# A recurrent tail walked by chunks, and attention's heads, softmax and value products placed inside the loop over cache pages

## The chip, the cores and the metric

The kernel runs on one core of one Trainium2 chip. The metric is the device time of one execution in microseconds (us); the median of several runs is compared. The engines are TensorE (PE; its weight loads are shown as PEld), VectorE (DVE), ScalarE (ACT), GpSimd (POOL) and SyncE (SP, which here only issues transfers). Each engine takes its instructions in a fixed order and waits on semaphores.

## What is computed

One inference step of a two-layer decoder for 256 prompt tokens and 8 sample tokens (T = 264 columns), model width 1024, all in float32. Layer 0 mixes by RWKV-7, layer 1 by latent attention, and after each a PEER expert mixer follows. Cut to what matters here:

```python
# layer 0, per head of 64, token by token (the kernel does it in 4 chunks of 64 tokens)
s = s*w_t - (s @ kk_t) * (kk_t*a_t) + v_t * k_t ;  y_t = s @ r_t
y = head_group_norm(y, ln_w, ln_b) + bonus ;  out = (y * g) @ w_out
# layer 1, prompt: 16 heads, two blocks of 128 queries, causal
o = softmax(scale*(q_nope k_nope^T + q_pe k_pe^T)) @ v
# layer 1, samples: 8 requests, each with 16 pages of 128 cached latents (256 wide) and keys (32 wide)
k_nope = rms_norm(ckv @ w_uk) * gain
s = scale*(q_nope . k_nope + q_pe . k_pe);  acc = softmax(s) @ ckv    # softmax over all pages and the new token
o = (acc/l) @ w_uv ;  out = o @ w_out
```

## The kernel before

Activations lie transposed, channels on partitions and the 264 tokens as columns, in 8 chunks of 128 channels. The weights stream through a ring of five tiles of 128x1024 (`ring`, 512 KB each), which SP loads in the order of use; an engine tells that a tile is free by `tile_used`. PSUM has eight banks of 128x512; TensorE's function `take(b)` waits until the last reader of bank b has raised `bank_free[b]`. `for_dve` and `for_act` tell a reader that a product is ready. `own` makes an engine wait for its own last instruction before it goes on, `tell` raises semaphores. `mm` (L714) and `turn` (a transpose, L773) issue TensorE's instructions; a float32 `mm` is two matmul instructions in the trace.

**Recurrent tail.** After the chunk products, `Pst` (the state of all 16 heads, 128x512) starts as chunk 0's. For each of chunks 1 to 3 TensorE makes 32 products of 64x64: for each half of the partitions what the old state adds to y, and then for each half the new state. The eight chunks c are walked inside one half. DVE adds the two y halves, then the two state halves, multiplies by the decay `lam`, and only then does the next chunk begin. Then come the group norm: head sums by a block matrix (8 products), centring on DVE, one square of all 128x2112 on DVE, head sums with 16 columns of weights (8 products), reciprocal and root, spreading back (8 products), gain, bias and gate on DVE over all chunks, and then the output product `rw_out` tile by tile with the sums of the next norm in it (`project_and_norm`).

**Prompt attention.** A loop of 17 turns over 16 heads: TensorE scores (4 products), DVE scale, mask and maximum, ACT two Exp, TensorE three `turn`s, ACT a copy, TensorE three value products, DVE the division. DVE prepares the masked query of the next head (`masked_query`). `o_row` is then turned back (16 `turn`s). After that TensorE makes the samples' query products (`qp`: 16 products with 16 columns, then 32 with 8), and only then may POOL load pages.

**Page loop.** 128 pages, 16 per request, four `cpT` buffers of the transposed page (192 KB, from `cache_t`), loaded by POOL when `page_used` tells that the page four earlier was scored. ACT rounds the page to its upper half (`page_upper`, two pages ahead), DVE makes the lower half (`page_lower`), TensorE makes the keys by 12 products of 512 columns into two banks, ACT squares both banks (`squares`), DVE sums the squares by head (`page_sums`) and copies the scores, which TensorE makes with the page as weights and 16 columns (3 products).

**Softmax and values.** After the last page: one root over all `SS` (128x2048), scores scaled, maxima over partitions (by a `turn` and a spread through a ones matrix), Exp, sums. Then 128 value products of 32 columns of weights by 256 columns, each with a natural page (`cpN`, 16 slots, 128 KB, from `cache_n`, issued in part by POOL and in part by ACT), copies of the rows on DVE, and 16 products that fold the rows back. Then `w_uv`, the output product `mla_out`, and layer 1's PEER.

Of the kernel before, what the change touches and what calls it, by code (L numbers as in the profile page):

```python
# [28 lines left out]
P = 128  # L29
# [3 lines left out]
NS = 8  # L33
# [136 lines left out]
def build(nc, x_t, shift_t, vecs, consts, wmasks, rope, wstream, sub_keys, mla_w, page_table, cache_t, cache_n,  # L170
          state, y_out, ckv_out, kpe_out, wkv_p_out, shift_out, wkv_s_out):
    ctx = ExitStack()
    with ctx:
# [103 lines left out]
        Pst = mis[:, 256:256 + 512].rearrange("p (c v) -> p c v", c=DC)  # L277
# [29 lines left out]
        def halves(name, cols, at):  # L307
# [70 lines left out]
        w_uv = A(2 * D, 2, D)  # L378
        w_ukT = A(DC * KVL, DC, KVL)
# [4 lines left out]
        qn_at = top[0]  # L384
        qn = A(N3, DC, T)
        kn_at = top[0]
        kn = A(N3, DC, T)
        qr = A(4 * T, 4, T)
        sqb = A(N3, DC, T)
        rs8 = A(N3, DC, T)  # L390
        vr_at = top[0]
        vr = A(2 * D, 2, D)
        o_t = A(N3, DC, T)
        qm = [A(512, 2, 256) for _ in range(2)]
        Sm = [A(384) for _ in range(2)]
        PTs = [A(384) for _ in range(2)]
        mxl = [A(8) for _ in range(2)]
        o_row = A(2 * D, 2, D)
# [10 lines left out]
        sqp = [o_row[:, j, :] for j in range(2)]  # L409
        small = A(10 * P, 10, P)  # L410
        cpT = [x.rearrange("p (a b) -> p a b", a=3) for x in Sm + PTs]
# [3 lines left out]
        acc_row = SS.rearrange("p g h -> p (g h)").rearrange("p (r n) -> p r n", r=NS)  # L415
        fold = small[:, 7, 0:HEADS]
        PR = rs8.rearrange("p c t -> p (c t)")[:, 0:NPG].rearrange("p (g h) -> p g h", h=HEADS)
        cpN = [a[:, i * KVL:(i + 1) * KVL] for a in (sqb.rearrange("p c t -> p (c t)"),
                                                     w_ukT.rearrange("p c n -> p (c n)")) for i in range(8)]

        uk_hi, uk_lo = halves("uk_hi", 2 * D, vr_at), halves("uk_lo", 2 * D, kn_at)
        pg_hi, pg_lo = halves("pg_hi", 4 * KVL, qn_at), halves("pg_lo", 4 * KVL, qn_at + 4 * KVL)
# [54 lines left out]
        yg_ready = sem("yg_ready")  # L477
        x_added = sem("x_added")
# [53 lines left out]
        rows_ready = sem("rows_ready")  # L532
        oall_ready = sem("oall_ready")

# [62 lines left out]
        def _(pool):  # L597
# [62 lines left out]
            pool.dma_start(wkv_p_out, Pst).then_inc(wkv_sent, 16)  # L660
# [13 lines left out]
            for n in range(4):  # L674
                page(pool, cache_t, n, cpT[n].rearrange("p a b -> p (a b)"), page_in[n])
            with pool.Fori(1, PAGES // 4) as it:
                for n in range(4):
                    pool.wait_ge(page_used, it * 4 + (n - 3))
                    page(pool, cache_t, it * 4 + n, cpT[n].rearrange("p a b -> p (a b)"), page_in[n])

            for n in POOL_SLOTS:
                page(pool, cache_n, n, cpN[n], natp_in[n])
            with pool.Fori(1, PAGES // NSLOT) as it:
                for n in POOL_SLOTS:
                    pool.wait_ge(natp_used, it * NSLOT + (n + 1 - NSLOT))
                    page(pool, cache_n, it * NSLOT + n, cpN[n], natp_in[n])
# [11 lines left out]
        def _(pe):  # L698
# [372 lines left out]
            for cc in range(1, NCH):  # L1071
                w.next(state_ready)
                cols = slice(cc * 64, cc * 64 + 64)
                for kind in range(2):
                    for h in range(2):
                        b = 2 * kind + h
                        take(b)
                        pr = slice(64 * h, 64 * h + 64)
                        for c in range(DC):
                            if kind == 0:  # L1080
                                last = mm(ps[pr, b, c * 64:(c + 1) * 64], Pst[pr, c, :], Rb[pr, c, cols])
                            else:
                                last = mm(ps[pr, b, c * 64:(c + 1) * 64], ETi[pr, c, cc, :], Pst[pr, c, :])
                        last.then_inc(for_dve, 1)

            w.next(ysm_back, 16)
# [6 lines left out]
            w.next(stat_ready)  # L1093
            head_roots(tmp_t, rs_rw)
            w.next(yg_ready)
            project_and_norm(TILES["rw_out"], y_t)
# [51 lines left out]
            for i in range(HEADS + 1):  # L1148
                if i < HEADS:
                    s, c = i % 2, i // 2  # L1150
                    w.next(qm_ready)
                    take(s)
                    for j in range(2):
                        o = ps[:, s, j * P:j * P + (j + 1) * P]
                        mm(o, qm[s][:, 0, j * P:(j + 1) * P], kn[:, c, 0:(j + 1) * P], True, False)
                        last = mm(o, qm[s][:, 1, j * P:(j + 1) * P], kp[:, 0:(j + 1) * P], False, True)
                    last.then_inc(for_dve, 1)
                if i >= 1:
                    h = i - 1
                    s = h % 2  # L1160
                    w.next(p_ready)
                    take(2 + s)
                    for k in range(3):
                        last = turn(ps[:, 2 + s, k * P:(k + 1) * P], Sm[s][:, k * P:(k + 1) * P])
                    last.then_inc(for_act, 1)
                    w.next(pt_ready)
# [71 lines left out]
            for n in range(PAGES):  # L1238
                req, p = n // NPAGE, n % NPAGE
                r = req % 2  # L1240
                if p == 0:
                    take(r)
# [1126 lines left out]
```

## Time and profile before

| | |
|---|---|
| runs | 3033.13, 3048.67, 3045.79 us; median 3045.79 |
| profiled execution | 3036.44 us, of which the profile's span is 3034.8 us |
| PE busy | 2768.0 us, 91% of the span |
| DVE busy | 1833.6 us, 60% |
| ACT busy | 1261.5 us, 42% |
| chain that ended last | PE 87%, DVE 6%, issue 2%, ACT 2%, DMA 1% |

The durations in the text are of the profiled execution. Granted clock means the share of full speed that TensorE was given: 1.00 is 2.4 GHz and 0.50 is 1.2 GHz; a value between is a mean over a stretch with both.

### The profile page before, as it was taken

The page shows a single profiled execution, that of the slowest core. Times are in us where ns is not written, and L with a number is a line of the kernel's source. Part 1 is how long each engine was busy: PE and PEld are TensorE (multiplying, and loading weights), DVE is VectorE, ACT ScalarE, POOL GpSimd, SP SyncE. Part 2 cuts the span into 40 slices and gives each one's busy share as a digit, 9 for nine tenths or more (in the row PEclk, how much of TensorE's full clock was granted, in tenths as well). Part 3 has the DMA queues.
Part 4 walks back from the last instruction along what each step waited for, and adds up shares of the span by engine and source line. Part 5 has one row for each costly group of instructions (what it writes and reads, how often), then busy time and mean ns, then how long its engine had stood idle before and what let it go on. Part 6 is the DMA issues. An engine that isn't in the chain of part 4 may idle for free.

```text
span 3034.8 us, 60374 instructions
## 1 busy us (share of the span) xinstructions
PE 2768.0 (91%) x22131; PEld 2522.1 (83%) x22131; DVE 1833.6 (60%) x3435; ACT 1261.5 (42%) x2565; POOL 181.6 (6%) x248
## 2 busy tenths in 40 slices
PE   8988699999999999975699999947999999999998
PEld 5777589999999999953488888822899999999998
DVE  5566457989985555525334444450579899855554
ACT  2333014467764444411233434410134677644443
POOL 0054000000000000000011111112000000000000
PEclk9999599999999999996689999975999999999999
DMA  4310034444445555530011122134345444455554
GB/s 163 120 43 27 15 119 152 162 163 157 160 148 181 182 182 180 205 144 0 1 42 57 57 58 58 57 89 135 121 150 167 160 154 160 148 182 182 181 180 139
DMA packets 112530, 378.00 MB, mean 125 GB/s; under 512 B 14617, under 2 KB 24090, under 8 KB 111842
## 3 DMA queue, kind: packets, MB, share of 16 engines
q1 hardware_dynamic: 88562, 322.17, 31.9%
q0 software_dynamic: 13424, 43.98, 4.9%
q10 hardware_dynamic: 10368, 9.44, 1.0%
q8 instruction: 119, 1.95, 0.3%
q14 instruction: 57, 0.47, 0.1%
HBM read 371.52 MB, written 4.01 MB: 124 GB/s over the span
## 4 chain that ended last, share of the span: by engine, by line
PE 87%; DVE 6%; issue 2%; ACT 2%; ACTq 1%; DMA 1%; DVEq 0%; POOLq 0%; POOL 0%; SPq 0%
PE ps L714 85%; DVE arena L1285 2%; ACT arena L1935 1%; DVE arena L1289 1%; ACTq L541 1%; DMA arena<-in_cache_n 1%; PE ps L1013 1%; PE ps L1008 1%; ACTq L542 0%; DVE ring_lo L1285 0%; PE ps L773 0%; DVE arena L1799 0%; ACT w_hi L1935 0%; DMA ring<-in_wstream 0%; DVE arena L1802 0%
## 5 line engine op out<-in xcount | busy, mean ns | idle before, releaser
L1285 DVE TENSOR_TENSOR ring_lo<-ring,w_hi 128x1024 fp32r<-128x1024 f32 x512 | 625.5, 1224 | 416.7 <-ACT w_hi L1935 413.3
L1935 ACT ACTIVATE arena<-ps 128x256 f32<-128x256 f32 (+19 forms) x981 | 397.5, 425 | 904.2 <-PE ps L714 823.5
L1935 ACT ACTIVATE w_hi<-ring 128x1024 fp32r<-128x1024 f32 x512 | 541.8, 1059 | 389.0 <-PE ps L714 388.6
L714 PE MATMUL ps<-arena 64*64 64x64 f32 (+11 forms) x5228 | 500.1, 275 | 143.4 <-DVEq L1282 54.6
L714 PE MATMUL ps<-x_hi,w_hi 128*128 128x264 f32 x2048 | 596.7, 291 | 15.5 <-DVE ring_lo L1285 15.5
L714 PEld LDWEIGHTS ps<-arena 64*64 64x64 f32 (+6 forms) x5228 | 391.5, 159 | 254.0 <-DMA arena<-in_cache_n 57.2
L714 PE MATMUL ps<-h_hi,w_hi 128*128 128x264 f32 x2048 | 580.1, 283 | 6.8 <-DVE ring_lo L1285 6.8
L714 PE MATMUL ps<-x_hi,ring_lo 128*128 128x264 f32 x2048 | 586.3, 286 | 0.0
L714 PE MATMUL ps<-x_lo,w_hi 128*128 128x264 f32 x2048 | 586.0, 286 | 0.0
L714 PE MATMUL ps<-h_lo,w_hi 128*128 128x264 f32 x2048 | 582.3, 284 | 0.0
L714 PE MATMUL ps<-h_hi,ring_lo 128*128 128x264 f32 x2048 | 581.9, 284 | 0.0
L1285 DVE TENSOR_TENSOR arena<-arena 128x512 f16<-128x512 f16 (+19 forms) x711 | 405.8, 590 | 46.8 <-ACTq L1940 31.3
L714 PEld LDWEIGHTS ps<-x_hi,w_hi 128*128 128x128 f32 x2048 | 390.7, 191 | 16.4 <-issue 16.3
L714 PEld LDWEIGHTS ps<-h_hi,w_hi 128*128 128x128 f32 x2048 | 385.7, 188 | 7.2 <-DVE ring_lo L1285 7.2
L714 PEld LDWEIGHTS ps<-x_lo,w_hi 128*128 128x128 f32 x2048 | 390.6, 191 | 0.0
L714 PEld LDWEIGHTS ps<-x_hi,ring_lo 128*128 128x128 f32 x2048 | 388.6, 190 | 0.0
L714 PEld LDWEIGHTS ps<-h_hi,ring_lo 128*128 128x128 f32 x2048 | 385.7, 188 | 0.0
L714 PEld LDWEIGHTS ps<-h_lo,w_hi 128*128 128x128 f32 x2048 | 385.7, 188 | 0.0
L714 PE MATMUL ps<-arena,ring 128*128 128x264 f32 (+2 forms) x1416 | 347.7, 404 | 25.3 <-DVE arena L1300 10.6
L714 PEld LDWEIGHTS ps<-arena,ring 128*128 128x128 f32 (+2 forms) x1416 | 275.4, 198 | 87.2 <-issue 20.1
L1935 ACT ACTIVATE arena<-arena 128x128 f16<-128x128 f16 (+5 forms) x586 | 200.2, 413 | 227.7 <-DVE arena L1289 121.2
L1849 DVE TENSOR_REDUCE arena<-arena 128x1024 f32 (+1 forms) x128 | 156.1, 1220 | 227.8 <-ACT arena L1935 227.8
(158 smaller groups left out, 2296.4 us busy)
## 6 DMA issues: line engine op xcount, KB each, us to landing
ring<-in_wstream SPq DMA_DIRECT2D x608, 512.0 KB, 3.3
arena<-in_cache_t POOLq DMA_DIRECT2D x128, 192.0 KB, 2.6
arena<-in_cache_n ACTq DMA_DIRECT2D x72, 128.0 KB, 2.4
arena<-in_cache_n POOLq DMA_DIRECT2D x56, 128.0 KB, 2.7
arena<-in_mla_w POOLq DMA_DIRECT2D x1, 3072.0 KB, 10.3
arena<-in_state POOLq DMA_DIRECT2D x4, 512.0 KB, 4.8
out_wkv_s<-arena POOLq DMA_DIRECT2D x4, 512.0 KB, 5.2
arena<-in_consts SPq DMA_DIRECT2D x1, 1408.0 KB
```

The source lines that it names most:

```text
L541: phys = eng.value_load(ptab[0:1, bass.ds(at, 1)], min_val=0, max_val=POOL - 1)
L714: return nc.tensor.matmul(out, lhsT, rhs, start=start, stop=stop, **kw)
L1008: last = nc.tensor.matmul(ps[par[f], 6 + x, q * CH:(q + 1) * CH], q4(XTs[x])[par[f], q, :], q4(Zs[x])[par[f], q, :], **acc)
L1013: last = nc.tensor.matmul(ps[par[f], 2 + x, q * CH:(q + 1) * CH], q4(Zs[x])[par[f], q, :], q4(XTs[x])[par[f], q, :], **acc)
L1285: return v.tensor_tensor(out, a, b, op)
L1289: v.reciprocal(x, x).then_inc(rsq_in, 1)
L1849: v.tensor_reduce(SS[:, bass.ds(at, 1), :].rearrange("p o h -> p (o h)"), sqp[n % 2].rearrange("p (h d) -> p h d", h=HEADS), AX.X, ALU.add ...
L1935: return nc.scalar.activation(out, in_, func, **kw)
```

## The change

Nothing of what is computed changes; order and placement do.

- The tail keeps a `Pst` for each chunk. Product by product it alternates between the two partition halves, puts both halves into one bank, and makes the new state first; reads of older states are placed behind it. DVE takes both halves in one operation. The norm goes chunk by chunk: ACT squares each chunk, and spreading, gain, bias, gate and the first four tiles of `rw_out` go by chunk, with four banks open at once.
- The samples' query products come before the heads. The 16 heads are taken one per page into the first 17 pages, in banks 6 and 7. All loops over pages are unrolled.
- Roots, maxima, Exp and sums go by request: while request r+1's pages are made, steps of request r stand at fixed pages p of the 16.
- Value products take the natural page as weights (two of 128x128, 16 columns moving), 23 pages behind the keys; the last request's stand after the loop. POOL now issues all pages, natural ones from when `o_ready` is told. The fold is gone.

TensorE's part of the tail, cut:

```diff
+            def new_state(cc):
+                w.next(state_ready)
+                take(3)
+                for c in range(DC):
+                    for pr in par:
+                        last = mm(ps[pr, 3, c * 64:(c + 1) * 64], ETi[pr, c, cc, :], Pst[cc - 1][pr, c, :])
+                last.then_inc(for_dve, 1)
...
+            new_state(1)
+            read_state(1, range(DC // 2))
+            new_state(2)
+            read_state(1, range(DC // 2, DC))
+            new_state(3)
...
+            read_state(2, range(DC))
+            read_state(3, range(DC))
...
+            for c in range(DC):
+                w.next(yg_ready)
+                for o in range(4):
+                    last = mm(ps[:, o, 0:T], wts[o][:, c, :], y_t[:, c, :], c == 0, c == DC - 1)
+                    if c == DC - 1:
+                        last.then_inc(tile_used, 1)
+                if c + 4 < DC:
+                    spread(c + 4)
```

TensorE's loop over pages:

```diff
+            for n in range(PAGES):
+                req, p = n // NPAGE, n % NPAGE
+                q = req - 1
+                pe.wait_ge(page_in[n % 4], 16 * (n // 4 + 1))
+                pe.wait_ge(pg_ready, n + 1)
+                take(2 * (n % 2))
+                half_keys(n, 0)
+                if q >= 0:
+                    if p == 2:
+                        turn_max(q)
+                    if p == 4:
+                        spread_max(q)
+                    if p == 7:
+                        prob_sums(q)
+                if q >= 1 and p < 7 and req < NS:
+                    page_values(q - 1, p + 9)
+                if q >= 0 and p >= 7:
+                    if req < NS - 1:
+                        page_values(q, p - 7)
...
+                half_keys(n, 1).then_inc(keys_made, 1)
+                if 1 <= n <= HEADS:
+                    head_turns(n - 1)
+                if n < HEADS:
+                    head_scores(n)
+                page_scores(n)
+                if 1 <= n <= HEADS:
+                    head_values(n - 1)
+            turn_max(NS - 1)
```

DVE's, ACT's and POOL's (`req`, `p` and `q` as above):

```diff
+            for n in range(PAGES):
...
+                if n + 2 < PAGES:
+                    page_lower(n + 2)
+                if n < HEADS:
+                    head_scores(n)
+                if 1 <= n <= HEADS:
+                    head_values(n - 1)
+                    if n == HEADS:
+                        tell(o_ready)
+                page_sums(n)
+                if n + 1 < HEADS:
+                    masked_query(n + 1)
+                if q >= 0:
+                    if p == 0:
+                        key_roots(q)
+                    if p == 1:
+                        request_scores(q)
+                    if p == 2:
+                        spread_max(q)
+                    if p == 4:
+                        shift_scores(q)
+                    if p == 6:
+                        prob_sums(q)
+                    if p == 7:
+                        inverse_sums(q)
+                if q >= 1 and p == 6:
+                    request_out(q - 1)
...
+            for n in range(PAGES):
...
+                if n + 2 < PAGES:
+                    page_upper(n + 2)
+                if q >= 0:
+                    if p == 1:
+                        root(of_req(SS, q))
+                    if p == 5:
+                        request_probs(q)
+                squares(n)
+                if 1 <= n <= HEADS:
+                    head_copy(n - 1)
+                if n < HEADS:
+                    head_probs(n)
...
+            for n in range(20):
+                page_keys(n)
+            pool.wait_ge(o_ready, 1)
+            for n in range(8):
+                page_rows(n)
+            for n in range(20, PAGES):
+                page_keys(n)
+                page_rows(n - 12)
```

`key_roots` is a scale and a reciprocal of 128x256 on DVE; `request_scores` two products of 128x256 and a maximum over the request's pages; `shift_scores` the subtraction of the maximum; `prob_sums` the sum over pages, then a product with ones; `request_out` reads the values' bank 7, adds the new token and divides.

```diff
+            def turn_max(q):
+                w.next(m1_ready)
+                take(6)
+                turn(ps[0:HEADS, 6, 0:P], sm(0, q)).then_inc(chain_made, 1)
...
+            def page_values(q, k):
+                n = q * NPAGE + k
+                if k == 0:
+                    w.next(pr_exp)
+                    take(7)
+                pe.wait_ge(natp_in[n % NSLOT], 16 * (n // NSLOT + 1))
+                for c in range(2):
+                    last = mm(ps[:, 7, c * HEADS:(c + 1) * HEADS], cpN[n % NSLOT][:, c * P:(c + 1) * P], PR[q][:, k, :],
+                              k + c == 0, k + c == NPAGE, skip_group_check=True)
+                last.then_inc(natp_used, 1)
```

## Rows read from the trace of the kernel before

**Rows 1.** Busy time by stage: us, busy us and instructions of each engine, granted clock, DMA.

```profile
310.10:336.60 26.50, 18.88 (x200) 18.32 (x200) 11.25 (x17) 0.00 (x0) 0.17 (x1) 0.50 0.01 1
336.60:369.40 32.80, 20.08 (x48) 11.86 (x48) 17.63 (x28) 0.42 (x1) 0.40 (x1) 0.60 0.02 8
...
1410.40:1518.60 108.20, 66.05 (x272) 52.57 (x272) 42.08 (x142) 23.60 (x80) 0.00 (x0) 0.67 0.00 1
1518.60:1545.50 26.90, 20.87 (x113) 20.78 (x113) 5.22 (x13) 4.71 (x6) 1.94 (x4) 0.56 0.06 16
1545.50:1984.70 439.20, 439.20 (x2300) 375.21 (x2300) 209.79 (x381) 175.60 (x254) 71.85 (x132) 1.00 0.21 58
1984.70:2023.50 38.80, 2.67 (x12) 1.77 (x10) 30.57 (x13) 7.61 (x6) 0.00 (x0) 0.57 0.10 30
2023.50:2115.00 91.50, 66.56 (x289) 19.79 (x288) 7.00 (x18) 0.00 (x0) 26.76 (x49) 0.63 0.56 161
1525.00:1539.00 14.00, 14.00 (x72) 14.00 (x71) 0.74 (x2) 0.08 (x1) 0.00 (x0) 0.53 0.00 0
```

**Rows 2.** The recurrent tail in order of time: start, us, engine, line, operation.

```profile
310.90 5.96 PE L714 MATMUL ps<-arena 64*64 64x64 f32 x64 [2.97 <-DVEq L1282]
...
318.57 0.69 DVE L1285 TENSOR_TENSOR arena<-arena 128x512 f32<-128x512 f32 x1
...
336.61 6.21 PE L714 MATMUL ps<-arena 128*128 128x264 f32 x16 [1.92 <-DVEq L1282]
...
346.15 6.46 PE L714 MATMUL ps<-arena 128*16 128x264 f32 x16 [3.32 <-DVE arena L1285]
...
355.57 7.40 PE L714 MATMUL ps<-arena 16*128 16x264 f32 x16 [2.96 <-DVEq L1282]
...
383.69 3.72 PE L714 MATMUL ps<-arena,ring 128*128 128x264 f32 x16
```

**Rows 3.** One page of the page loop in order of time.

```profile
1704.21 0.74 PE L714 MATMUL ps<-arena 128*128 x6
1704.56 1.02 ACT L1935 ACTIVATE arena<-ps 128x1024 f32<-128x1024 f32 x1 [2.03 <-PE ps L714]
...
1705.73 1.22 DVE L1849 TENSOR_REDUCE arena<-arena 128x1024 f32 x1 [1.84 <-ACT arena L1935]
...
1706.87 0.18 DVE L1852 COPY arena<-ps 128x32 f32 x1
```

**Rows 4.** One head of the heads loop in order of time.

```profile
1433.80 0.17 DVE L1807 RECIPROCAL arena<-arena 128x2 f32<-128x2 f32 x1 [3.31 <-PE ps L714]
...
1434.75 0.35 DVE L1788 TENSOR_SCALAR arena<-arena 128x256 f32<-128x256 f32 x1
...
1436.22 0.85 PE L773 MATMUL ps<-cst,arena 128*128 128x128 f32 x3
...
1436.47 0.56 DVE L1799 SCALAR_TENSOR_TENSOR arena<-ps,arena 128x384 f32<-128x384 f32 x1 [1.09 <-PE ps L714]
...
1438.02 0.40 ACT L1935 ACTIVATE arena<-arena 128x128 f32<-128x128 f32 x1 [5.90 <-DVE arena L1803]
```

**Rows 5.** After the page loop, in order of time.

```profile
1988.52 12.95 DVE L1289 RECIPROCAL arena<-arena 128x2048 f32<-128x2048 f32 x1
1994.58 1.28 ACT L1935 ACT_TABLE_LOAD   x1 [8.71 <-issue]
...
2003.45 2.29 DVE L1868 SCALAR_TENSOR_TENSOR arena<-arena 128x2048 f32<-128x2048 f32 x1 [1.98 <-ACT arena L1935]
...
2008.10 3.57 DVE L1873 TENSOR_REDUCE arena<-arena 128x128 f32<-128x2048 f32 x1
...
2105.72 6.64 PE L714 MATMUL ps<-arena 128*128 128x16 f32 x32 [0.69 <-DVEq L1282]
```

**Rows 6.** POOL's page transfers: one issue of the timeline, and the landing times.

```profile
1981.07 0.55 POOL L542 DMA_DIRECT2D arena<-in_cache_n  x1 [0.59 <-issue]
...
arena<-in_cache_t POOLq DMA_DIRECT2D x128, 192.0 KB, 2.6
```

More of the change, by code:

```diff
@@ new lines, in _ @@
+                page_scores(n)
+                if 1 <= n <= HEADS:
+                    head_values(n - 1)
+            turn_max(NS - 1)
+            for j in range(2):
+                for half in range(2):
+                    b = 2 * j + half
+                    take(b)
+                    for c in range(4):
+                        cc = half * 4 + c
+                        last = turn(ps[:, b, c * P:(c + 1) * P], o_row[:, j, cc * P:(cc + 1) * P])
+                    last.then_inc(for_act, 1)
@@ L1253, in _ @@
+            spread_max(NS - 1)
+            for k in range(NPAGE):
+                page_values(NS - 1, k)
+            prob_sums(NS - 1)
             w.next(acc_ready)
@@ L1747, in _ @@
+            tell(root_ready)
+            for c in range(DC):
+                y_c = y_t[:, c, :]
+                w.next(for_dve)
+                own(v.scalar_tensor_tensor(y_c, y_c, V("ln_w", c), ps[:, 4 + c % 4, 0:T], ALU.mult, ALU.mult))
+                tell(bank_free[4 + c % 4])
+                own(v.scalar_tensor_tensor(y_c, y_c, V("ln_b", c), bon_t[:, c, :], ALU.add, ALU.add))
+                tt(y_c, y_c, g_t[:, c, :], ALU.mult).then_inc(yg_ready, 1)
             residual(TILES["rw_out"])
@@ new lines, in head_values, with key_roots @@
+            def head_values(h):
+                s = h % 2
+                w.next(head_o)
+                own(v.reciprocal(mxl[s][:, 6:8], mxl[s][:, 4:6]))
+                for j in range(2):
+                    own(v.tensor_scalar(o_row[:, j, h * 64:(h + 1) * 64], ps[:, 7, 384 + j * 64:384 + (j + 1) * 64],
+                                        mxl[s][:, 6 + j:7 + j], None, ALU.mult))
+                tell(bank_free[7])
+            def key_roots(q):
+                own(v.tensor_scalar(of_req(SS, q), of_req(SS, q), 1.0 / 64, EPS, ALU.mult, ALU.add))
+                v.reciprocal(of_req(SS, q), of_req(SS, q)).then_inc(rsq_in, 1)
@@ L1911, in _ @@
+            key_roots(NS - 1)
+            request_out(NS - 2)
+            request_scores(NS - 1)
+            spread_max(NS - 1)
+            shift_scores(NS - 1)
+            prob_sums(NS - 1)
+            inverse_sums(NS - 1)
+            request_out(NS - 1)
             tell(acc_ready)
@@ L2172, in _ @@
                     solve(x)
+            for c in range(DC):
+                w.next(cen_ready)
+                fn(tmp_t[:, c, :], y_t[:, c, :], ACT.Square).then_inc(sqc_ready, 1)
             root(rs_rw)
@@ new lines, in _, with page_upper, squares @@
+            fn(uk_hi[:, :].rearrange("p (c n) -> p c n", c=2), w_uk).then_inc(ukhi_ready, 1)
+            def page_upper(n):
+                act.wait_ge(page_in[n % 4], 16 * (n // 4 + 1))
+                fn(pg_half[0][:, n % 4], cpT[n % 4][:, 0:2, :]).then_inc(pghi_ready, 1)
+            def squares(n):
+                b = 2 * (n % 2)
+                w.next(keys_made)
+                act.wait_ge(sqp_used, n + 1)
+                own(fn(sqp[n % 2].rearrange("p (a n) -> p a n", a=2), ps[:, b:b + 2, :], ACT.Square))
+                tell(sqp_ready, bank_free[b])
```

494 lines of the change are left out of this document (212 added, 282 removed).

## The prediction

> **What bounds it now.** The page and the chain of waits say that TensorE is busy for 91% of the span, so the question is where it isn't, and where it works at its low clock. I read the busy time by stage next [rows 1]. The page loop (439.2 us) is TensorE's alone: busy throughout, granted clock 1.00, 3.43 us a page; DVE is busy 48% and ACT 40% of it. Around it lie stages that no engine fills: the heads (108.2 us, TensorE busy 61%, clock 0.67), softmax (38.8 us, DVE's), values (91.5 us, paced by POOL's and ACT's transfers). In layer 0 the tail's state steps (26.5 us at clock 0.50) and norm (32.8 us) alternate between two engines. The timelines give the prices inside [rows 2 to 6]. PEER, the larger part of the span, isn't touched.
>
> **The tail.** A chunk step takes 8.4 us now, from 310.90 to the end of DVE's multiply at 319.26 [rows 2]: 5.96 of 32 products, then DVE. After, only the new state is in the circle: 16 products, 3.0 us if they stay one behind another, 1.5 if the two partition halves run side by side, which the alternation allows; I take 1.5. Then two operations of 0.69 and about 0.5 of handover: 3.5 us, three times 10.6. The reads of states 2 and 3 and their additions come behind it, about 3.4. So 14 us for 25.7, a gain of 11.7 (6 if the halves don't overlap). The norm's three product groups start at 336.61, 346.15 and 355.57 [rows 2]. The square leaves the path between the first two, as ACT does it by chunk beside the products: 7.1 for eight at the low clock, then 6.5 at once, and 3.0 for the roots, 16.6 for 19.0. TensorE then works 13 us without a break, so I expect part of it at the high clock, and take 13.5: a gain of 5.5. From the spreads to the output product are 13.8 us (355.57 to 369.4). By chunk, the first gate is ready after 2.8 (a product, then DVE's three operations of one chunk); four spreads move into the product for 0.47 to 0.9 each (3.72 for eight at the high clock, 7.40 at the low [rows 2]), and tile 5 waits 0.9 for the residual addition that frees bank 0. Gain 7.6. DVE needs about 1.6 us a chunk there and TensorE 2.3, so DVE doesn't set the pace. Its fifth to seventh tiles load only when the first four are all through; the fifth's own 3.7 us hide the first landing. Tail: **-25** (-15 to -31).
>
> **The heads' stage goes.** 108.2 us [rows 1]. The query products' stage (26.9) keeps its length: it loses the 16 turns, gains DVE's preparation of the queries, which now nothing hides, and its 16-column products start at the low clock. **-108.**
>
> **Heads in the page loop.** TensorE's work for a head at the high clock: four score products of 128 and 256 columns, 1.4 by the 264-column pace; three turns, at most 0.5 (0.85 at the low clock [rows 4]); three value products of the shape of the page's scores, three for about 0.69: a page is 3.43, and its twelve key products leave that. Together 2.5, so 5.9 us a page if all waits are covered. They aren't. Count from K, the end of a page's keys. Scores end at K+1.8. DVE starts 0.35 later, and needs 1.5 until the exponentials may start (1436.47 to 1438.02 [rows 4]): K+3.6. Next on DVE stands `head_values` with 0.95 (1433.80 to 1434.75): K+4.6. Then `page_sums`, 1.22 and 0.18 [rows 3] and two handovers: K+6.1. Only then `masked_query`, twice 0.35: K+6.8. TensorE would want the next scores at K+6.2 and gets them at K+6.8, so the cycle is DVE's, 6.5 us for 3.43. Extra 3.07 x 16 and 1 for the last: **+50** (at TensorE's pace +40; if each head costs the present 6.8 us over and above the page, +108). TensorE's gap stays below 1 us, so I count with the high clock.
>
> **Softmax and values leave the end.** From the last keys to `w_uv` are 130.4 us (1984.7 to 2115.0). What remains is the last request's chain. DVE: sums to K+3.1, reciprocal of an eighth of 12.95 with its scale to K+5.2 [rows 5]; `request_out` of the request before stands in front of the scores, 0.9; then an eighth of 2.29 twice and of 3.57, with fixed costs 1.5: K+7.7. TensorE's queue stands at `turn_max` till then, with the 16 turns of `o_row` behind it: 3.7, to K+11.6. Spread, shift, a table load, Exp: K+14.5. Then 32 value products; 16 with 16 columns took 6.64 at the low clock [rows 5], 72 instructions, which are 36 products, 14.0 [rows 1]: 12.5. Sum and `request_out` 1.9. In all 29: **-101** (-94 to -107).
>
> **Values in the loop.** 112 pages with two products like the three of the page's scores, 0.23 each at the high clock: **+51.5**. By the low-clock rows a product is 0.39 to 0.42: +90. POOL issues a page in 1.14 [rows 6], two are 2.3 in a page of 3.9, and natural pages lie 14 pages ahead, so no transfer is waited for in steady state.
>
> **New waits of each request.** This term has no row of its own. K0 is the end of the keys of a request's first page. `key_roots` is ready at K0+5.2; ACT's root, about 0.4, stands before `squares` of the next page, which therefore start at K0+5.7 and not K0+4.2; DVE's sums of them end at K0+8.3, and `request_scores` only then: `m1_ready` at K0+9.9. TensorE's queue comes to `turn_max` at K0+5.5 (first request) or K0+6.0, with all later keys behind it: it stands **4.0 to 4.5 us**. `spread_max` and the exponentials have two pages and are in time. `prob_sums` on DVE at p = 6 is ready 3.8 after that page's keys, and TensorE asks at 2.1: 1.7. The first value product waits for `request_out` on DVE, 0.3. About 6.1 a request, 43 for seven (0 if DVE and ACT get ahead, 80 if each of both points waits a page more). The chain's own small products, 4. One delay at `o_ready`: POOL issues eight natural pages, 9 us, before page 20's transposed one, which lands 2.6 later [rows 6]; TensorE has three pages for that, and ACT's `page_upper(20)` holds up `squares(18)`: 2. After a stand of 4 us TensorE may go on at the low clock (after the gap of 3.32 us before 346.15 it did: 6.46 for eight products [rows 2]); 3 us each time, in a third of the cases: 7. Together **+56**.
>
> ACT must change tables twice a request, for the root and for Exp, 14 changes more than now. A load takes 1.28, and the one at 1994.58 runs while the root still waits for DVE [rows 5]; both places in the loop have such idle time (1.3 to 2 us before the wait ends), so the sum has nothing for them but the one at the end. The Trainium skill, "ScalarE: Activation LUTs", section "What ACT_TABLE_LOAD costs", speaks against so many changes: it gives about 2.66 us for each with a drain. By that, `squares` at p = 5 would come 0.6 later, which the bank two pages on still covers, and the end would be 1.4 longer; the trace shows the 1283 ns and no drain, since no work stands behind it.
>
> **Sum.** -25 - 108 + 50 - 101 + 51.5 + 56 = -76.5. The profiled execution took 3036.4: 2960. Its time lies 9 below the median of the three runs, inside their spread of 15; I give 2 for that: **2962 us**. The spread of 0.5% is what a measurement of this kernel can tell from no change.
>
> **Rivals.**
> - *The waits are covered.* DVE and ACT are less than half busy in the loop [rows 1], and my chain stacks every handover. Then heads cost 40 and the requests' points perhaps 10 instead of 50 with the clock: 2962 - 10 - 40 = 2912. Against: `m1_ready` is behind a reciprocal of 1.7, a root and a full page's sums in one queue, whatever the handovers. 0.22.
> - *Heads aren't overlapped.* The circle DVE, ACT, TensorE of a head takes 6.8 us alone (108.2/16). If the page's squares and sums sit inside it instead of beside it, heads cost 108, and the request points about 70: 2962 + 58 + 20 = 3040, no change. Against: in the order of the loop the page's keys lie between each head's stages. 0.10.
> - *The clock falls in the loop: slower.* With weights of 128x128 and 16 columns moving TensorE was busy for 14.0 of 14.0 us and granted 0.53 [rows 1]. Such products are three of fifteen in a page now and will be five of seventeen, with stands beside them. A page of 3.9 us would become about 7.3 at the low clock. It decides against the change when 24 of the 128 pages run so (76.5 + 6 over 3.4); at a third of them, 43, the time is 2962 + 146 = 3108. Against: three of fifteen left the clock at 1.00 for 439 us. The Trainium skill, "TensorE: Matmul & The Clock Gate", says the gate goes by how busy the PE has been; by that alone the loop would stay high, and the row at 0.53 shows that busy isn't all. 0.06.
> - *The tail gains twice as much or nothing* moves the time by 25 at most and is inside the range.
>
> **How the numbers follow.** The forecast 0.62, around it 2930 to 2995. Covered waits 0.22, no overlap 0.10, clock 0.06. The range 2905 to 3010 takes in the first rival and the forecast's upper bounds (values at 0.3 a product, points at 80) and leaves out the two others, 0.16, and a little below. Faster by over 0.5% (below 3030): 0.62 + 0.22 and half of no overlap: 0.89. Within 0.5%: 0.05. Slower: 0.06.
>
> **What would show it.** Right: gaps of about 4 us on TensorE before the one-instruction `turn` at the third page of each request, released by DVE, and of 1.7 at the eighth; 6.5 us a page for the first 16, released by DVE's masked query; 3.9 a page else at clock 1.00; 29 us from the last keys to `w_uv`; state steps of 3.5 us. Wrong: a clock under 0.95 over the loop, waits for `in_cache_n` in it, or a head page above 8 us.

## The result, and the profile after

The changed kernel takes 3005.13 us (median of 9 runs, 2996.75 to 3019.90), the kernel before beside it 3035.05 us (9 runs, 3026.55 to 3048.67). The ratio is 0.9895, 95% interval 0.9878 to 0.9911: 32 us faster by the ratio, 30 by the medians. The forecast was 2962. The direction is right and the time is inside the range, but less than half of the expected gain of 76.5 came.

From the first page of the profile after: TensorE's busy time, and in 40 slices its busy tenths and granted clock (one slice is 75 us; the page loop lies in slices 19 to 28).

```profile
span 3001.5 us, 59707 instructions
...
PE   8977899999999999976989999998999999999998
...
PEclk9999999999999999986989998887999999999999
```

In the loop TensorE is busy nearly all the time, and yet the clock's digits in its last four slices are 8, 8, 8 and 7. In the kernel before, the loop's clock was 1.00 [rows 1]. So the next view is the busy time by request, each stretch from DVE's page sums of a request's first page to those of the next request's: the stretch and its length, then busy us of TensorE, its weight loads, DVE, ACT, POOL, the granted clock, the DMA share and GB/s.

```profile
1520.60:1593.80 73.20, 66.90 (x332) 56.40 (x331) 35.02 (x62) 24.55 (x35) 21.86 (x40) 0.88 0.31 87
1593.80:1667.20 73.40, 67.96 (x358) 57.87 (x357) 35.47 (x64) 26.36 (x37) 17.48 (x32) 0.93 0.26 72
1667.20:1739.50 72.30, 66.86 (x359) 56.91 (x358) 35.49 (x64) 26.36 (x37) 17.48 (x32) 0.95 0.25 74
...
1811.80:1890.30 78.50, 73.06 (x359) 61.97 (x358) 35.54 (x65) 26.36 (x37) 17.49 (x32) 0.87 0.24 68
...
1968.70:2049.60 80.90, 74.89 (x361) 63.92 (x360) 32.80 (x60) 24.08 (x33) 19.63 (x36) 0.83 0.23 67
```

A request took 54.7 us before, 16 pages of 3.42 by the distance of their page sums (3.43 by the loop's 439.2 us [rows 1]). It takes 72.3 to 80.9 now. The columns of DVE and ACT do not change from request to request and are below half, so neither is short of time. TensorE's idle part is 5.4 us in most requests (6.3 in the first), and from the third to the seventh its busy part grows from 66.9 to 74.9 with the same number of instructions (358 to 361) while the clock goes from 0.95 to 0.83. With the lower level at 0.50, a mean of 0.95 over 72.3 us is about 7 us there (twice the missing 5%), and 0.83 over 80.9 is about 27. The idle part is named by the waits of TensorE over requests two to six (us in total, times, the longest):

```profile
PE ps L792 <- DVEq L1371: 18.7, 5, 3.7
PE ps L733 <- DVEq L1371: 7.4, 5, 1.5
```

Line 792 is `turn`, so the first is `turn_max` at the third page, once in each request; the second is `prob_sums` at the eighth. These are the two gaps that the prediction named. What leads to the first one, in order of time, in the third request:

```profile
1669.27 1.75 DVE L1958 RECIPROCAL arena<-arena 128x256 f32<-128x256 f32 x1
...
1671.06 0.42 ACT L2072 ACTIVATE arena<-arena 128x256 f32<-128x256 f32 x1 [1.99 <-DVE arena L1958]
...
1671.38 1.01 ACT L2072 ACTIVATE arena<-ps 128x1024 f32<-128x1024 f32 x1
...
1672.47 1.22 DVE L1929 TENSOR_REDUCE arena<-arena 128x16 f32<-128x1024 f32 x1 [1.16 <-ACTq L2077]
...
1674.17 0.42 DVE L1964 SCALAR_TENSOR_TENSOR arena<-arena 128x256 f32<-128x256 f32 x1
...
1675.09 0.58 DVE L1966 TENSOR_REDUCE arena<-arena 128x16 f32<-128x256 f32 x1
...
1675.78 0.28 PE L792 MATMUL ps<-cst,arena 128*16 128x128 f32 x1 [3.74 <-DVEq L1371]
...
1677.04 0.63 PE L733 MATMUL ps<-uk_hi,pg_lo 128*128 128x512 f32 x1
```

This is the chain as the prediction stacked it: the reciprocal, ACT's root in front of the page's squares, the page's sums in front of the request's scores. The last row is new: the key product behind the gap takes 0.63 us, and its neighbours start 0.42 to 0.43 apart. Ahead of the gap the same product takes 0.39 at a distance of 0.23. Stretches of 3 us around the gap of the sixth request show how long this lasts there:

```profile
1895.00:1898.00 3.00, 0.06 (x1) 0.00 (x0) 2.19 (x4) 0.83 (x2) 1.09 (x2) 1.00 0.36 108
1898.00:1901.00 3.00, 2.20 (x8) 2.01 (x9) 1.08 (x3) 0.00 (x0) 0.00 (x0) 0.56 0.01 4
1901.00:1904.00 3.00, 3.00 (x11) 2.61 (x11) 0.26 (x1) 1.17 (x2) 0.00 (x0) 0.50 0.00 0
...
1907.00:1910.00 3.00, 3.00 (x14) 2.58 (x14) 0.00 (x0) 0.61 (x1) 0.00 (x0) 0.73 0.16 47
1910.00:1913.00 3.00, 3.00 (x16) 2.31 (x16) 1.84 (x3) 0.83 (x2) 0.55 (x1) 1.00 0.20 38
```

A clock of 0.50 is the lower level, 1.2 GHz. This gap of 3.7 us is followed by about 10 us there, and work that runs there for 10 us would have been done in 5. So this gap costs 3.7 by itself and 5 behind it. It isn't the same for all. In the third request the stretch at the lower level is 6.8 us long; in the fourth there are two of 3.4, one behind each gap; in the seventh, 17 us follow the gap of 1.5:

```profile
1676.60:1683.30 6.70, 6.70 (x23) 5.63 (x21) 2.34 (x5) 1.44 (x2) 1.09 (x2) 0.50 0.12 30
1748.30:1751.50 3.20, 3.20 (x11) 2.67 (x10) 0.21 (x1) 0.00 (x0) 0.00 (x0) 0.50 0.02 5
1772.20:1775.40 3.20, 3.20 (x10) 2.66 (x10) 0.42 (x1) 0.00 (x0) 0.00 (x0) 0.50 0.08 26
...
2004.30:2021.20 16.90, 16.90 (x56) 14.58 (x57) 4.60 (x10) 2.88 (x4) 2.19 (x4) 0.50 0.14 36
```

Over the seven requests the clock falls twelve times behind fourteen gaps: behind every gap at `turn_max`, and behind the 1.5 us at `prob_sums` in five requests, not in the second and third. In all some 109 us are at the lower level.

The other stages did what was forecast. The recurrent tail, answering to [rows 2] (start, us, what):

```profile
315.28 0.69 DVE L1374 TENSOR_TENSOR arena<-arena 128x512 f32<-128x512 f32 x1 [0.34 <-DVE arena L1790]
...
316.07 1.61 PE L733 MATMUL ps<-arena 64*64 64x64 f32 x48 [2.99 <-DVEq L1371]
...
318.84 1.61 PE L733 MATMUL ps<-arena 64*64 64x64 f32 x48 [1.16 <-DVE arena L1374]
...
321.62 1.15 PE L733 MATMUL ps<-arena 64*64 64x64 f32 x32 [1.17 <-DVE arena L1374]
...
326.36 7.49 PE L733 MATMUL ps<-arena 128*128 128x264 f32 x32 [1.00 <-DVEq L1371]
...
336.81 2.27 PE L733 MATMUL ps<-arena 16*128 16x264 f32 x8 [2.96 <-DVEq L1371]
...
339.31 3.86 PE L733 MATMUL ps<-arena,ring 128*128 128x264 f32 x8 [0.23 <-DVE arena L1374]
```

A chunk step is 2.8 us (316.07 to 318.84 to 321.62) for 8.4. In this execution the steps ran at clock 1.00, and in the kernel before at 0.50 [rows 1]. And the end, answering to [rows 5]:

```profile
2049.59 1.22 DVE L1929 TENSOR_REDUCE arena<-arena 128x16 f32<-128x1024 f32 x1 [1.87 <-ACTq L2077]
...
2055.64 3.56 PE L792 MATMUL ps<-cst,arena 128*16 128x128 f32 x17 [6.62 <-DVEq L1371]
...
2061.97 13.63 PE L733 MATMUL ps<-arena 128*128 128x16 f32 x64 [2.46 <-ACT arena L2072]
...
2077.55 2.65 PE L733 MATMUL ps<-arena 128*64 128x8 f32 x46 [1.52 <-DVEq L1371]
```

From the sums of the last page to the product with `w_uv` are 28.0 us.

**The sum, stage by stage**, measured between the same instructions in the profiled executions (3034.8 and 3001.5 us):

| Stage | before | after | difference | forecast |
|---|---|---|---|---|
| unchanged work up to the tail | 310.1 | 315.3 | +5.2 | 0 |
| tail to layer 0's PEER | 103.5 | 72.6 | -30.9 | -25 |
| PEER of layer 0, projections | 996.9 | 996.5 | -0.4 | 0 |
| query products, heads' stage | 135.0 | 26.7 | -108.3 | -108 |
| pages 0 to 15, with the 16 heads | 61.0 | 109.5 | +48.5 | +50 |
| pages 16 to 127: values, chains, gaps, clock | 379.4 | 529.0 | +149.6 | +107.5 |
| last page's sums to `w_uv` | 129.1 | 28.0 | -101.1 | -101 |
| unchanged rest | 919.8 | 924.0 | +4.2 | 0 |
| all | 3034.8 | 3001.5 | -33.3 | -76.5 |

The first and last rows are the same instructions in both kernels; in the nine profiled executions other than the changed kernel's the first of them lay between 306.7 and 314.8. One term is off from the forecast by more than that: the requests' 112 pages, by 42 us.

### The profile page after: what moved, and what is told of

Its sections match the earlier page's. It is cut to its first block, busy times and chain, and to the rows that moved or that the text cites. A ratio compares the mean times of both kernels' runs of the same rounds, so it can differ in the third digit from the quotient of the medians.

```text
span 3001.5 us, 59707 instructions
## 1 busy us (share of the span) xinstructions
PE 2789.8 (93%) x22390; PEld 2577.9 (86%) x22390; DVE 1864.9 (62%) x3534; ACT 1292.3 (43%) x2607; POOL 221.0 (7%) x319
## 4 chain that ended last, share of the span: by engine, by line
PE 87%; DVE 8%; issue 2%; ACT 2%; DMA 0%; DVEq 0%; POOL 0%; ACTq 0%; POOLq 0%; SPq 0%
PE ps L733 85%; DVE arena L1929 2%; DVE arena L1374 1%; ACT arena L2072 1%; DVE arena L1378 1%; PE ps L1032 1%; PE ps L1027 1%; DVE arena L1958 0%; DVE ring_lo L1374 0%; PE ps L792 0%; DVE arena L1951 0%; DVE arena L1939 0%; ACT w_hi L2072 0%; DVE arena L1932 0%; DVE arena L1892 0%
## 5 line engine op out<-in xcount | busy, mean ns | idle before, releaser
L2072 ACT ACTIVATE arena<-ps 128x256 f32<-128x256 f32 (+18 forms) x981 | 396.9, 424 | 964.5 <-PE ps L733 886.4
L733 PEld LDWEIGHTS ps<-arena 64*64 64x64 f32 (+4 forms) x5452 | 440.8, 160 | 157.3 <-DVEq L1371 45.4
L733 PE MATMUL ps<-arena 64*64 64x64 f32 (+11 forms) x5452 | 483.0, 252 | 89.1 <-DVEq L1371 49.7
L1374 DVE TENSOR_TENSOR arena<-arena 128x512 f16<-128x512 f16 (+18 forms) x741 | 410.4, 573 | 49.0 <-ACTq L2077 31.3
L1929 DVE TENSOR_REDUCE arena<-arena 128x16 f32<-128x1024 f32 x128 | 156.1, 1220 | 240.7 <-ACTq L2077 238.2
L2072 ACT ACTIVATE arena<-arena 128x128 f16<-128x128 f16 (+5 forms) x615 | 207.0, 406 | 152.0 <-DVE arena L1378 68.3
## 6 DMA issues: line engine op xcount, KB each, us to landing
arena<-in_consts POOLq DMA_DIRECT2D x1, 1408.0 KB, 13.8
```

Source lines behind the costliest of these rows:

```text
L733: return nc.tensor.matmul(out, lhsT, rhs, start=start, stop=stop, **kw)
L1374: return v.tensor_tensor(out, a, b, op)
L1929: own(v.tensor_reduce(SS[:, n, :], sqp[n % 2].rearrange("p (h d) -> p h d", h=HEADS), AX.X, ALU.add))
L2072: return nc.scalar.activation(out, in_, func, **kw)
```

## The experiments

**The points moved later.** Theory 1 is that the gaps before the two waits set both the idle time and the low clock; the rival is that the clock falls because of the narrow value products. The first edit moves `turn_max` and `prob_sums` a page later and the root behind the page's squares, and shifts what hangs on them. Everything is still computed.

```diff
-                    if p == 2:
+                    if p == 3:
                         turn_max(q)
-                    if p == 4:
+                    if p == 5:
                         spread_max(q)
-                    if p == 7:
+                    if p == 8:
                         prob_sums(q)
-                if q >= 1 and p < 7 and req < NS:
-                    page_values(q - 1, p + 9)
+                if q >= 1 and p == 0:
+                    page_values(q - 1, 9)
+                if q >= 1 and p < 6:
+                    page_values(q - 1, p + 10)
...
-                    if p == 1:
-                        root(of_req(SS, q))
...
                 squares(n)
+                if q >= 0 and p == 1:
+                    root(of_req(SS, q))
```

> The request's steps each stand one page later than the step they wait for is ready (turn_max at p=3, spread_max at p=5, prob_sums at p=8, root behind squares, request_out at p=5, values of a request end at p=5). Theory 1 (gaps cost themselves and the low clock behind them): both gaps of a request, 3.7 to 4.2 and 1.5 us, go, and with them the stretches of about 10 us at granted clock 0.5; a request's 16 pages take 62 to 63 us instead of 72 to 78, the loop is about 85 us shorter and the time 2915 to 2930 us. Rival (the low clock comes from the narrow products, 16 columns moving over 128x128 weights): only the gaps go, 38 us, the clock in the loop stays at 0.82 to 0.95, time 2960 to 2975.

Measured: 2922.70 us (2918.68 to 2925.58), ratio to the kernel before 0.9624 (0.9596 to 0.9652), so 82 us faster than the changed kernel. TensorE has no wait left in requests two to six, and the windows by request are:

```profile
1522.90:1590.80 67.90, 62.79 (x336) 53.35 (x335) 34.87 (x62) 25.83 (x36) 21.85 (x40) 0.95 0.32 94
1590.80:1653.90 63.10, 63.10 (x358) 54.41 (x358) 35.47 (x64) 26.36 (x37) 17.48 (x32) 1.00 0.29 84
1653.90:1717.00 63.10, 63.10 (x358) 54.40 (x358) 35.39 (x64) 26.36 (x37) 17.48 (x32) 1.00 0.30 84
```

63.1 us of work in 63.1 us at clock 1.00, with the value products in: 8.4 more than the 54.7 before for 32 value products and the request's small ones, where the prediction had 7.4 and 0.6. This prices the values, and it prices the gaps with all that follows them at 9 to 19 us a request from the second on. In the first it is only 5.3, because there TensorE now waits 5.0 us for ACT, which POOL's late page 20 holds up.

**The tail alone.** The tail's part of the change in the kernel before, attention as it was:

```diff
+            new_state(1)
+            read_state(1, range(DC // 2))
+            new_state(2)
+            read_state(1, range(DC // 2, DC))
+            new_state(3)
...
```

> Only the recurrent tail of the change, attention as before. Both theories: the tail is worth the 31 us between the first state multiply and layer 0's PEER that the traces show, ratio 0.990 (3004 us beside 3035). Rival: the 5 us that the chunk products before the tail take longer in the trace of after belong to the tail change, then 0.9915.

Measured: 3011.75 us (3008.67 to 3013.96), ratio 0.9919 (0.9891 to 0.9947), 24 us. The trace's marks give -30.9 for the tail, as in the changed kernel; the time gives -16 to -33. The tail is worth what the stage table says, within what a run can tell, and does nothing to the loop: 54.72 us a request. The rival had the 5 us ahead of the tail belong to this change. This execution does reach the tail late, at 314.4 us, but seven others with the same tail reach it at 306.7 to 314.8, on both sides of the 310.1 before, so that isn't shown to be the tail's; the median of 24 alone would not tell the two apart.

With ten profiled executions side by side, the tail has a second form. In five of the nine with the new tail (this one, the changed kernel's and three more) its state steps run at the high clock, in the other four at the low one. Here are TensorE's rows of a low one, from the kernel with only the first gap taken away (below):

```profile
312.79 2.01 PE L733 MATMUL ps<-arena 64*64 64x64 f32 x48 [2.99 <-DVEq L1371]
315.56 2.83 PE L733 MATMUL ps<-arena 64*64 64x64 f32 x48 [0.76 <-DVE arena L1374]
319.16 1.97 PE L733 MATMUL ps<-arena 64*64 64x64 f32 x32 [0.78 <-DVE arena L1374]
```

A step is then 3.6 us (315.56 to 319.16), and the tail 2.5 to 2.9 us longer: from its first multiply to the product behind the wait of 3.55 it takes 67.6 to 67.7 in the five, 70.2 to 70.6 in the four, and 98.6 in the kernel before. So the new tail gives 28 to 31 us.

**No value products.** This kernel leaves out the value products of 14 of a request's 16 pages; the samples' attention is computed from the rest alone. The gaps stay.

```diff
             def page_values(q, k):
...
+                if k not in (0, NPAGE - 1):
+                    pe.sem_inc(natp_used, 1)
+                    return
```

> Of each request's 16 pages only the first and the last page's value products are made, the others are left out; waits and order stay. Theory 1: the gaps at turn_max and prob_sums stay, and so do the stretches at clock 0.5 behind them (mean granted clock of a request's pages 0.95 or less); a page at the high clock falls by 0.45 us, a request by about 6.5. Rival (narrow products lower the clock): the clock of the loop from the second request on returns to 0.98 or more although the gaps stay.

Measured: one run, 2915.57 us.

```profile
1578.70:1648.30 69.60, 63.72 (x303) 53.09 (x302) 35.49 (x64) 26.34 (x37) 17.48 (x32) 0.90 0.26 76
1648.30:1719.00 70.70, 64.81 (x303) 53.94 (x302) 35.49 (x64) 26.36 (x37) 17.49 (x32) 0.88 0.26 75
1719.00:1783.90 64.90, 59.02 (x303) 49.43 (x302) 35.49 (x64) 26.36 (x37) 17.48 (x32) 0.97 0.29 82
```

With no more narrow products in most pages than the kernel before had, the clock still fell, in three requests to 0.88 to 0.92. So the value products are not needed for the fall. In the last four requests it was 0.97, better than with them. The gaps here are 4.2 and 1.5 us. Whether fewer narrow products make the low stretches shorter, or they only fall differently from one request to the next, this run leaves open.

**The gaps filled.** The sharpest test: add work. Three more halves of a page's keys are made before `turn_max` and one before `prob_sums` (the same products again into the same bank, 24 a request), and no wait is moved.

```diff
                     if p == 2:
+                        for _ in range(3):
+                            half_keys(n, 1)
                         turn_max(q)
...
                     if p == 7:
+                        half_keys(n, 1)
                         prob_sums(q)
```

> The changed kernel with its gaps filled: before turn_max TensorE makes the six wide products of the page's second half three times more, and before prob_sums once more, into the bank that they are written to anyway. No wait goes, work is added. Theory 1 (the low clock is the price of the standing, and the larger part of it): the clock stays at 0.98 or more, a request takes 68 to 70 us instead of 72 to 80, the time falls to 2955 to 2970 us. Rival (the narrow products, or something else than the gaps, lower the clock, or the gaps cost only themselves): the added work costs nothing or up to 10 us, the clock in the requests stays at 0.83 to 0.95, time 3000 to 3015.

Measured: 2956.76 us (2948.82 to 2960.26), ratio 0.9727 (0.9691 to 0.9763).

```profile
1590.30:1659.70 69.40, 69.08 (x383) 58.94 (x382) 35.61 (x64) 26.46 (x37) 17.53 (x32) 1.00 0.27 77
```

24 more instructions of TensorE in a request, and a request of 69.4 us instead of 72.3 to 78.5. DVE and ACT do what they did, in the same chain. The useless work takes the idle time's place, and the clock stays at 1.00. Over the seven requests it is 483.1 for 529.0, 46 us less in the profiled executions and 48 in the medians. The fill is about 1 us a request longer than the gaps (69.4 for 63.1 of work and 5.2 of gaps), so the low clock by itself costs some 53.

**Only the first gap taken away.** `turn_max` at p = 3 and the root behind the squares, but `prob_sums` left where it was on DVE and TensorE.

```diff
-                    if p == 2:
+                    if p == 3:
                         turn_max(q)
-                    if p == 4:
+                    if p == 5:
                         spread_max(q)
                     if p == 7:
                         prob_sums(q)
...
```

> Only the wait for the maximum is taken out (turn_max at p=3, spread_max at p=5, root behind squares); the gap of 1.5 us at prob_sums stays. If that short gap alone never lowers the clock, each request takes 63.1 + 1.6 = 64.7 us at clock 1.00 and the time is about 2935. If it lowers it, requests take up to 70 us, clock 0.9 to 0.95, time 2950 to 2970.

Measured: one run, 2949.14 us. The wait of TensorE that is left, then the windows of the second, third and fourth request:

```profile
PE ps L733 <- DVEq L1371: 9.7, 6, 1.6
```

```profile
1588.70:1654.10 65.40, 63.57 (x359) 54.45 (x358) 35.49 (x65) 26.36 (x37) 17.49 (x32) 1.00 0.28 81
1654.10:1722.60 68.50, 66.67 (x358) 56.98 (x357) 35.34 (x64) 26.36 (x37) 17.48 (x32) 0.95 0.27 78
1722.60:1791.10 68.50, 66.67 (x358) 56.97 (x358) 35.47 (x64) 26.36 (x37) 17.48 (x32) 0.95 0.27 78
```

The same gap of 1.6 us stands in each. In the second request the clock stays at 1.00 and the request takes 65.4; in the third to fifth it falls and they take 68.5, 3.1 more. In the sixth the fall costs 1.6, in the seventh about 7. So a gap of 1.6 us is enough to lower the clock, and it does not do so each time. What decides between the cases was not settled. It isn't chance from one execution to the next alone: the changed kernel and the next two experiments below, which all have the same gaps, show the same clocks in requests two to seven, 0.93, 0.95, 0.95, 0.87, 0.87 and 0.83.

**The heads' next query first.** DVE makes `masked_query(n + 1)` before `head_values(n - 1)` and the page's sums.

```diff
                 if n < HEADS:
                     head_scores(n)
+                if n + 1 < HEADS:
+                    masked_query(n + 1)
                 if 1 <= n <= HEADS:
                     head_values(n - 1)
...
                 page_sums(n)
-                if n + 1 < HEADS:
-                    masked_query(n + 1)
```

> DVE makes the masked query of the next head before it divides the last head's output and sums the page's squares. My count of the heads' cycle: a head page falls from 6.37 us to TensorE's own 5.8 or 5.9, since the query then is ready 2 us before TensorE asks, and the first 16 pages are 8 us shorter. Rival (ACT's p_ready or the copy of the turned probabilities sets the cycle): stays at 6.3.

Measured: one run, 2987.93 us; a page with a head takes 5.78 us, 6.36 in the changed kernel. Over 16 heads that is 9 us. The rest of the difference to 3005 is not the edit's: this execution reached the tail at 306.7 us, the changed kernel's at 315.3. What stood in front of the query in the changed kernel is seen in DVE's timeline of one page:

```profile
1425.24 0.60 DVE L1951 TENSOR_SCALAR arena<-ps,arena 128x64 f32<-128x64 f32 x2
1425.99 1.22 DVE L1929 TENSOR_REDUCE arena<-arena 128x16 f32<-128x1024 f32 x1
1427.35 0.19 DVE L1932 COPY arena<-ps 128x32 f32<-128x32 f32 x1
1427.69 0.35 DVE L1892 TENSOR_SCALAR arena<-arena 128x256 f32<-128x256 f32 x1
1427.96 0.35 DVE L1893 TENSOR_SCALAR arena<-arena 128x256 f32<-128x256 f32 x1
```

**Keys ahead of natural pages.** POOL issues page 20's transposed page first, and two natural pages behind each from there.

```diff
-            for n in range(8):
-                page_rows(n)
+            row = 0
             for n in range(20, PAGES):
                 page_keys(n)
-                page_rows(n - 12)
+                while row <= min(n - 12, 2 * (n - 20) + 1):
+                    page_rows(row)
+                    row += 1
-            for n in range(PAGES - 12, PAGES):
+            for n in range(row, PAGES):
                 page_rows(n)
```

> GpSimd issues page 20's transposed page first when the heads are done, and two natural pages behind each transposed one, instead of eight natural pages first. My prediction priced the delay at 2 us; the trace of after shows one page of 9.02 us there where 3.5 to 3.9 is usual. If it is POOL's queue: that page falls to below 5 us, the first request by 7 to 10 us with the clock behind it. Rival (it is the maximum's wait of the first request): the page stays at 8 or more.

Measured: one run, 2995.16 us. The page around `turn_max` of the first request goes from 9.02 to 7.05 us, but the page behind it from 3.94 to 5.66, and the whole request only from 73.2 to 72.9. So in this order POOL's queue costs next to nothing: the delay lies beside the gap of 4.8 before `turn_max`, which stays. Both expectations missed, a page below 5 and a request shorter by 7 to 10. The 10 us to the changed kernel's time are not shown to be the edit's: this execution reached the tail at 309.6, 5.6 earlier. With the gap gone the same edit is worth more, as the next kernel shows.

**All of it together.** The points later, the query first, POOL's order, and the 16 turns of `o_row` put ahead of the last `turn_max`, which TensorE otherwise waits 6.6 us for.

```diff
-            turn_max(NS - 1)
             for j in range(2):
...
+            turn_max(NS - 1)
             spread_max(NS - 1)
```

> All that was found together: request steps later, masked query first, GpSimd's order, and the 16 turns of the heads' output ahead of the last turn_max. By the parts: 2922.7 less 9 for the heads, 5 for the page at 20 and 3 for the turns: 2900 to 2910 us.

Measured: 2896.74 us (2894.46 to 2906.79), ratio 0.9549 (0.9512 to 0.9587), 3 below the expected 2900 to 2910. Heads' pages take 5.78 us; the requests 60.6, five times 63.1, and 61.9. The first is 7.3 below that of the kernel with only the points moved (67.9): there POOL's eight natural pages made page 20 late and ACT with it, TensorE waited 5.0 us, and the low clock followed that gap too. From the last sums to `w_uv` are 24.9 us for 28.0. This is the fastest kernel here: 143 us below the kernel before, 108 below the changed one.

## Why the prediction was right in direction and wrong in size

**The step that failed** is the last one of the new waits: "After a stand of 4 us TensorE may go on at the low clock ...; 3 us each time, in a third of the cases: 7." The mechanism was named; its size was off by more than a factor of seven. What the low clock took, request by request: the measured time, less 60.6 or 63.1 or 61.9 of work (from the kernel with all edits), less the gaps (5.2; 6.3 in the first): 6.3, 5.1, 4.0, 4.0, 10.1, 10.1 and 13.8, in all 53, and the kernel with the gaps filled gives 53 too. Three things were wrong in it. The clock falls in every request, not in a third. The gap of 1.5 us was not thought of as one that can do it, while in five of the seven requests it did as well, which makes twelve falls and not two or three. And a fall costs about 4.5 us in the mean (half of its time at the lower level, 1.7 to 8.5), not 3. The 3 was a fair reading of its one row [rows 2]: the eight products from 346.15 on took 6.46 us, and the clock was back 0.9 us before they ended:

```profile
349.00:351.50 2.50, 2.50 (x7) 0.82 (x6) 0.00 (x0) 0.00 (x0) 0.00 (x0) 0.50 0.00 0
351.50:352.60 1.10, 1.10 (x5) 0.25 (x3) 0.00 (x0) 0.00 (x0) 0.00 (x0) 0.90 0.00 0
```

One row could not tell how far the stretches of the loop would differ. The 42 us add up: 46 more for the clock and 3 more for the values, 5 less for the gaps and 2 less for POOL.

**Right within 4 us**: the heads' stage (-108.3 for -108), the heads in the loop (+48.5 for +50, with 6.36 a page for 6.5, by DVE's masked query as said), the end (29.1 from the last keys for 29). The value products with the small ones are 58.6 for 55.5: the 0.23 of the page's scores carried over. The two gaps came where they were told, 3.7 for 4.0 to 4.5 (4.8 in the first request) and 1.5 for 1.7, together 37.6 for 43. **POOL's 2** did not come: no wait of TensorE in the changed kernel is POOL's, and its order alone moved the first request by 0.3. It became a wait of 5.0 only in the kernels without the first gap.

**The tail** gave 30.9 for 25. State steps were 26.5 us [rows 1] and are 11.1 (315.28 to 326.36), for 14: a step is 2.8 at the high clock and 3.6 at the low one, for which 3.5 was worked out. So the surplus is the clock's, which the forecast had not counted on there. The two halves did overlap, though not wholly: at the low clock 16 products take 1.97 us, 1.5 in the forecast, and 2.98 without it (half of 5.96 [rows 2]). The norm gives 8.5 for 5.5 (19.0 to 10.45); in the kernel with only the first gap taken away, one of the four with low steps, it is 12.5, and so 6.5. The spreads reach the output product in 2.5 us for 13.8, but the product's stage is then 4.4 longer with the spreads inside it: 7.0 net, forecast 7.6. In the four executions with the low clock in the steps, the three terms together are 28.

**The table loads** cost nothing in the loop, as the sum had it: each takes 1.28 us and stands in ACT's idle time, and the kernel with the points moved has all of them and, from its second request on, no wait of TensorE in the loop. By the Trainium skill, "ScalarE: Activation LUTs", section "What ACT_TABLE_LOAD costs", each would be about 2.66 with its drain. The traces show the load alone, also where work stands behind it: at the end of the loop Exp starts 0.01 us after the load, which starts 0.17 after ACT's instruction before.

**The rivals.** *Waits are covered*: false in this order; the kernel with the points moved is that case, and it took 2923 where the rival said 2912 (the heads stayed at DVE's pace, and POOL's delay of 5 appeared). *Heads aren't overlapped*: false, 6.36 a page. *The clock falls in the loop*: it did, to 0.83 to 0.95, which the prediction had put down as a sign that it was wrong. But it came by the gaps and not by the narrow products: at 1.00 with all of them and no gaps, at 0.88 to 0.92 in three requests without most of them. Each page at the low clock costs about 3.4, so 53 us are some 16 pages of 128, below the 24 from which the rival would have turned the sign. The Trainium skill, "TensorE: Matmul & The Clock Gate", section "What's actually happening", says the gate follows how busy the engine has been. The filled gaps agree, with 1.00 for 0.83 to 0.95.

## What to carry to other kernels

Where TensorE is the bound and runs at its high level, price a gap on it as the gap and, in the mean of this loop's fourteen, some 4 us behind it (0 to 8.5 for a single one), even a gap of 1.5 us, and count gaps before counting their length. A step that another engine prepares should be asked for a page later than it is ready, not at the first place where it might be. To see whether the clock is what a gap costs, fill it with work that is thrown away: if the kernel gets faster, it is.

## What was not expected of the hardware

- Adding 24 wide products to each request, with nothing taken away, made the kernel 48 us faster (2956.76 for 3005.13).
- A gap of 1.5 to 1.6 us in an engine otherwise busy at 1.00 was followed by the lower clock in most requests, but not in all (five of seven in the changed kernel, five of six with only the first gap taken away): 65.4 and 68.5 us for the same instructions. The gap of 2.99 us ahead of the tail's state steps was followed by it in four executions of nine.
- A gap of 3.7 us was followed by 3.4 to 10 us at 1.2 GHz (one of 1.5 us by up to 17), in which TensorE was busy all the time.
- Products of 64x64 in the two partition halves, issued in turn, overlapped in part: 16 of them in 1.97 us at the low clock, where 32 one half after the other took 5.96 [rows 2].
- Unchanged work ahead of the change took 306.7 to 315.3 us from one execution to another, as much as one of the smaller edits is worth.
